# na_in's attention scores as f32r products of high and low halves, the queries' norm moved to where the scores are read

## What is computed

```python
def _heads(h, w, g=None):
    t = (h @ w).reshape(b, n, -1, HEAD_DIM)          # 16 heads of 64
    return t if g is None else _rms(t, g)            # t * rsqrt(mean(t*t) + EPS) * g

# queries of 256 tokens, keys and values of 256 + 256 (context)
s_loc = einsum(q_r, k_win) * scale + bias            # scale = 64 ** -0.5
s_ctx = einsum(q_r, k_ctx) * scale
p = softmax(concatenate([s_loc, s_ctx], axis=-1))
out = p_loc @ v_win + p_ctx @ v_ctx
```

## Time and profile before

| | us |
|---|---|
| median of 3 runs | 1310.28 |
| lowest and highest run | 1308.92, 1313.0 |
| the profiled execution, own time | 1312.8 |
| its span, first to last instruction | 1310.7 |
| mean granted TensorE clock | 0.997 of full |

### The profile page before, as it was taken

The page is one execution under the profiler, slowest core; times in us unless marked ns, Lnnn a source line. Parts: engine busy times, 40 slices in busy tenths (PEclk is TensorE's granted clock), DMA queues, the critical chain, the costliest instruction groups (busy, mean ns, idle before and its releaser), DMA issues.

```text
span 1310.7 us, 19842 instructions
## 1 busy us (share of the span) xinstructions
PE 1292.8 (99%) x7748; PEld 1102.5 (84%) x7748; DVE 868.7 (66%) x1303; ACT 594.8 (45%) x955; POOL 430.9 (33%) x433
## 2 busy tenths in 40 slices
PE   9999999999999999999999999999999999999999
PEld 8887989999886888788788888887777777999987
DVE  6687688999966588798333543335667666855553
ACT  6236556666653223354311234223555554766432
POOL 1462232333320002365300244111457552488200
PEclk9999999999999999999999999999999999999999
DMA  8777566555655344554444444444522321655552
GB/s 302 238 266 255 170 204 203 183 181 189 199 187 209 137 160 137 177 180 163 155 145 145 145 145 145 141 147 162 193 80 98 113 81 54 203 178 184 187 192 81
DMA packets 66268, 219.97 MB, mean 168 GB/s; under 512 B 9120, under 2 KB 12448, under 8 KB 66176
## 3 DMA queue, kind: packets, MB, share of 16 engines
q1 hardware_dynamic: 65888, 218.46, 49.3%
q10 hardware_dynamic: 288, 0.25, 0.1%
HBM read 217.21 MB, written 1.05 MB: 167 GB/s over the span
## 4 chain that ended last, share of the span: by engine, by line
PE 76%; DVE 13%; issue 5%; ACT 3%; DMA 2%; POOL 1%; SPq 0%; DVEq 0%; ACTq 0%; POOLq 0%
PE ps L624 19%; PE ps L638 18%; PE ps L636 18%; PE ps L614 7%; PE ps L616 4%; DVE wlo L1713 4%; DVE tmp L2003 2%; DMA raw<-in_w_in 2%; PE ps L1074 1%; DVE Y L1740 1%; PE ps L1101 1%; PE ps L1088 1%; ACT A L1258 1%; PE ps L1067 1%; PE ps L739 1%
## 5 line engine op out<-in xcount | busy, mean ns | idle before, releaser
L624 PE MATMUL ps<-A,whi 128*128 128x256 f32 (+2 forms) x1564 | 513.0, 328 | 0.2 <-ACT A L1490 0.2
L638 PE MATMUL ps<-A,wlo 128*128 128x256 f32 (+2 forms) x1536 | 492.3, 320 | 2.1 <-DVE wlo L1713 2.1
L636 PE MATMUL ps<-A,whi 128*128 128x256 f32 (+2 forms) x1536 | 491.9, 320 | 0.2 <-DVE A L1726 0.2
L1713 DVE TENSOR_TENSOR wlo<-raw,whi 128x1024 fp32r<-128x1024 f32 (+1 forms) x302 | 393.3, 1306 | 88.4 <-ACT whi L1233 88.2
L1233 ACT ACTIVATE whi<-raw 128x1024 fp32r<-128x1024 f32 (+1 forms) x302 | 316.7, 1051 | 266.9 <-PE ps L638 137.6
L624 PEld LDWEIGHTS ps<-A,whi 128*128 128x128 f32 x1564 | 297.9, 190 | 43.4 <-issue 18.4
L638 PEld LDWEIGHTS ps<-A,wlo 128*128 128x128 f32 x1536 | 292.6, 191 | 23.9 <-DVE wlo L1713 2.9
L636 PEld LDWEIGHTS ps<-A,whi 128*128 128x128 f32 x1536 | 293.1, 191 | 22.0 <-issue 1.7
L2394 POOL TENSOR_TENSOR H<-tmp,H 128x256 fp32r<-128x256 f32 (+1 forms) x86 | 125.8, 1462 | 56.4 <-ACT H L1548 42.9
L614 PE MATMUL ps<-H,whi 128*128 128x512 f32 x400 | 140.3, 395 | 0.2 <-POOL H L2394 0.2
L616 PE MATMUL ps<-H,wlo 128*128 128x256 f32 x400 | 112.3, 281 | 0.6 <-DVE wlo L1713 0.6
(11 more groups left out here) (321 smaller groups left out, 1496.9 us busy)
## 6 DMA issues: line engine op xcount, KB each, us to landing
raw<-in_ada SPq DMA_DIRECT2D x96, 512.0 KB, 4.3
raw<-in_w SPq DMA_DIRECT2D x64, 512.0 KB, 3.5
raw<-in_w_up SPq DMA_DIRECT2D x44, 512.0 KB, 3.5
raw<-in_w_in SPq DMA_DIRECT2D x34, 512.0 KB, 5.7
raw<-in_w_0a SPq DMA_DIRECT2D x32, 512.0 KB, 3.7
raw<-in_w_0b SPq DMA_DIRECT2D x32, 512.0 KB, 3.5
raw<-in_na_in SPq DMA_DIRECT2D x24, 512.0 KB, 5.7
raw<-in_w_down SPq DMA_DIRECT2D x22, 512.0 KB, 3.5
```

The source lines that it names most:

```text
L624: e.matmul(o, w_hi, ah, start=k == 0, stop=False)
L636: e.matmul(o, w_hi, al, start=False, stop=False)
L638: m = e.matmul(o, w_lo, ah, start=False, stop=last)
L1713: e.tensor_tensor(wlo[i % NRAW][:, :cols], raw[i % NRAW][:, :cols], plain(whi[s % NHI][:, :cols]), SUB).then_inc(S("wlo").sem, 1)
```

## The change

The scores of a head are made from f32r halves. A tile q_both holds 512 columns: in the columns of head x its own 64 rows hold the high half of the unscaled queries, and the other 64 rows the low half. k_hi holds the high half of the head's keys in all 128 rows (the same values twice), k_lo the low half in the head's own rows and zeros in the others. One product with k_hi and one with k_lo, both 128 rows deep, give high by high, low by high and high by low.

The queries are no longer multiplied by their norm and gain. Both gains go into the keys (head_gain), and the queries' root is a column for the 128 queries of a block (query_scale): their sum of squares is taken with the squares as weights and two columns of the ones matrix, and the scale is applied where VectorE reads the scores. VectorE makes that root's Newton step itself on four columns.

ScalarE writes the high halves: two copies for the queries at their chunk, four for the keys three chunks later (keys_hi). VectorE subtracts the queries' low half from PSUM one chunk later (queries_lo), and the bank of a query chunk now waits for that too. GpSimd makes the keys' Newton step and scales the keys (key_newton) at the following chunk, and subtracts their low halves (keys_lo) three chunks later, in the program behind the key_newton of that place. k2 has two tiles in place of three. Before the stage, VectorE clears the other rows of k_lo and makes the two gain columns.

The diff, with comments and places of tiles cut:

```diff
...
     cv = h32("cv", 2048, 40960).rearrange("p (c t) -> p c t", c=4)
-    k2 = [h32(f"k2_{i}", 512, 2048 * i) for i in range(3)]
-    q2 = [h32(f"q2_{i}", 256, 6144 + 1024 * i) for i in range(3)]
+    k2 = [tmp[1], tmp[3]]
+    q_both = [sb(f"q_both{i}", 512, f32r, at=h_at + at) for i, at in enumerate((0, 2048, 4096))]
+    key_places = [51200 + 2048 * i for i in range(7)] + [6144]
+    k_hi, k_lo = [[[sb(f"{what}{c}{x}", 512, f32r, at=h_at + key_places[4 * c + 2 * y + x]) for x in range(2)] for c in range(2)]
+                  for y, what in enumerate(("k_hi", "k_lo"))]
     v2 = [h32(f"v2_{i}", 512, 9216 + 2048 * i).rearrange("p (t c) -> p t c", t=4) for i in range(3)]
...
             return None
-        return (2 * c, k2[c % 3], 512) if kind == "k" else (2 * c + 1, q2[c % 3], 256)
+        return (2 * c, k2[c % 2], 512) if kind == "k" else (2 * c + 1, q_both[c % 3], 256)
     turn2 = {}
...
                 turn2["scores", 4 * p + 2 * b + x] = len(turn2)
+    query_mean, head_gain = small[:, 24:28], small[:, 40:42]
+    key_mean, key_root = (tmp[0], rst), (tmp[2], ssum)
+    def query_scale(p):
+        return small[:, 28 + 4 * (p % 3):32 + 4 * (p % 3)]
+    def key_at(n):
+        return NA_CHUNKS[n][1] if 0 <= n < 24 and NA_CHUNKS[n][0] == "k" else None
+    def query_at(n):
+        return NA_CHUNKS[n][1] if 0 <= n < 24 and NA_CHUNKS[n][0] == "q" else None
     GROUPS = (range(5), range(5, 9), range(9, 13))
...
                 w.wait_ge(S(signal), count)
+                if name == "na_in" and query_at(n - 3) is not None:
+                    w.wait_ge(S("q_lo"), 2 * query_at(n - 3) + 2)
         def low_ready(s):
...
             w.wait_ge(S("na"), n + 1)
-            o = turn_bank("norm", j)[:, :T]
-            e.matmul(o, const("blocks"), src, start=True, stop=True).then_inc(S("hn_sum").sem, 1)
+            o = turn_bank("norm", j)
+            if j % 2 == 0:
+                e.matmul(o[:, :T], const("blocks"), src, start=True, stop=True).then_inc(S("hn_sum").sem, 1)
+                return
+            for b in range(2):
+                m = e.matmul(o[:, 2 * b:2 * b + 2], src[:, 128 * b:128 * b + 128], const("blocks")[:, 0:128:64],
+                             start=True, stop=True)
+            m.then_inc(S("hn_sum").sem, 1)
         def scores2(p, b):
-            w.wait_ge(S("hn_out"), 2 * p + 2)
+            w.wait_ge(S("k_hi"), 4 * p + 4)
+            w.wait_ge(S("k_lo"), 2 * p + 2)
+            w.wait_ge(S("q_lo"), 2 * p + 2)
+            w.wait_ge(S("key_zero"), 4)
             for x in range(2):
                 o = turn_bank("scores", 4 * p + 2 * b + x)
-                e.matmul(o, q2[p % 3][rows_of(x), 128 * b:128 * b + 128], k2[p % 3][rows_of(x), :],
-                         start=True, stop=True).then_inc(S("s2_mm").sem, 1)
+                both = q_both[p % 3][:, 256 * x + 128 * b:256 * x + 128 * b + 128]
+                e.matmul(o, both, k_hi[p % 2][x], start=True, stop=False)
+                e.matmul(o, both, k_lo[p % 2][x], start=False, stop=True).then_inc(S("s2_mm").sem, 1)
         def turned2(p, b):
...
         def head_root(j, T):
-            m, r = tmp[j % 2][:, :T], tmp[2 + j % 2][:, :T]
+            m, r = (query_mean, query_scale(j // 2)) if j % 2 else (key_mean[j // 2 % 2], key_root[j // 2 % 2])
             w.wait_ge(S("na_bank"), turn2["norm", j] + 1)
-            if j >= 2:
-                w.wait_ge(S("hn_out"), j - 1)
+            if j % 2 == 0 and j >= 4:
+                w.wait_ge(S("hn_out"), j // 2 - 1)
             e.activation(r, m, ACT.Ln).then_inc(S("hn_ln").sem, 1)
...
             e.activation(r, r, ACT.Exp, scale=-0.5).then_inc(S("hn_exp").sem, 1)
+        def keys_hi(c):
+            w.wait_ge(S("hn_out"), c + 1)
+            if c >= 2:
+                w.wait_ge(S("s2_mm"), 4 * (c - 2) + 4)
+            for x in range(2):
+                e.activation(k_hi[c % 2][x][rows_of(x)], k2[c % 2][rows_of(x)], ACT.Copy).then_inc(S("k_hi").sem, 1)
+            for x in range(2):
+                e.activation(k_hi[c % 2][x][rows_of(1 - x)], k2[c % 2][rows_of(x)], ACT.Copy).then_inc(S("k_hi").sem, 1)
         def exp2(p, b):
...
                     sqr = sq[j % 2]
-                    if c >= 3:
-                        w.wait_ge(S("s2_mm"), 4 * (c - 3) + 4)
-                    e.activation(dst, o[:, :T], ACT.Copy).then_inc(S("na_copy").sem, 1)
+                    if j % 2:
+                        if c >= 3:
+                            w.wait_ge(S("s2_mm"), 4 * (c - 3) + 4)
+                        for x in range(2):
+                            e.activation(dst[rows_of(x), half(x)], o[rows_of(x), :T], ACT.Copy).then_inc(S("q_hi").sem, 1)
+                    else:
+                        if c >= 2:
+                            w.wait_ge(S("k_lo"), 2 * c - 2)
+                        e.activation(dst, o[:, :T], ACT.Copy).then_inc(S("na_copy").sem, 1)
                     if c:
...
                     e.activation(tmp[4], o, ACT.Copy).then_inc(S("na").sem, 1)
+                if key_at(n - 3) is not None:
+                    keys_hi(key_at(n - 3))
             if what == "after":
...
             ada_place(i)
+        for c in range(2):
+            for x in range(2):
+                e.memset(plain(k_lo[c][x][rows_of(1 - x)]), 0.0).then_inc(S("key_zero").sem, 1)
+        for i, factor in enumerate((-0.5, 1.5)):
+            e.scalar_tensor_tensor(head_gain[:, i:i + 1], param("k_g"), factor, param("q_g"), MUL, MUL).then_inc(S("head_gain").sem, 1)
         def head_mean(j, T):
             w.wait_ge(S("hn_sum"), j + 1)
-            if j >= 2:
-                w.wait_ge(S("hn_rr"), j - 1)
             bank = ps[4 + turn2["norm", j] % 2]
-            e.tensor_scalar(tmp[j % 2][:, :T], bank[:, :T], 1.0 / 64, EPS, MUL, ADD).then_inc(S("na_bank").sem, 1)
-        def head_out(j, T, dst, gain):
-            c, kind = j // 2, j % 2
-            w.wait_ge(S("hn_rr"), j + 1)
-            w.wait_ge(S("na_copy"), j + 1)
-            e.scalar_tensor_tensor(dst, dst, gain, tmp[2 + j % 2][:, :T], MUL, MUL).then_inc(S("hn_out").sem, 1)
+            if j % 2:
+                if j > 1:
+                    w.wait_ge(S("hn_q"), j // 2)
+                e.tensor_scalar(query_mean, bank[:, 0:4], 1.0 / 64, EPS, MUL, ADD).then_inc(S("na_bank").sem, 1)
+                return
+            if j >= 4:
+                w.wait_ge(S("hn_out"), j // 2 - 1)
+            e.tensor_scalar(key_mean[j // 2 % 2], bank, 1.0 / 64, EPS, MUL, ADD).then_inc(S("na_bank").sem, 1)
+        def queries_lo(c, n):
+            o, into = bank_of("na_in", n), q_both[c % 3]
+            w.wait_ge(S("q_hi"), 2 * c + 2)
+            w.wait_ge(S("na"), n + 1)
+            for x in range(2):
+                e.tensor_tensor(into[rows_of(1 - x), half(x)], o[rows_of(x), :256], plain(into[rows_of(x), half(x)]),
+                                SUB).then_inc(S("q_lo").sem, 1)
+        def query_newton(c):
+            m, r = query_mean, query_scale(c)
+            w.wait_ge(S("hn_exp"), 2 * c + 2)
+            for _ in range(2):
+                e.tensor_tensor(m, m, r, MUL).then_inc(own.sem, own.up())
+                w.wait_ge(own, own.n)
+            e.tensor_scalar(m, m, -0.0625, 0.1875, MUL, ADD).then_inc(own.sem, own.up())
+            w.wait_ge(own, own.n)
+            e.tensor_tensor(r, r, m, MUL).then_inc(S("hn_q").sem, 1)
         def values_out(c):
...
                 m = small[:, 8 + 4 * i:9 + 4 * i]
+                scale = query_scale(p)[:, 2 * b + x:2 * b + x + 1]
+                w.wait_ge(S("hn_q"), p + 1)
                 w.wait_ge(S("s2_mm"), j + 1)
...
                 bank = ps[4 + turn % 2]
-                e.scalar_tensor_tensor(X[x][:, 0:256], bank[:, 0:256], 0.125, bt[h % 4][:, b], MUL, ADD).then_inc(S("na_bias").sem, 1)
-                e.tensor_scalar(X[x][:, 256:512], bank[:, 256:512], 0.125, None, MUL, ALU.bypass).then_inc(S("na_bank").sem, 1)
+                e.scalar_tensor_tensor(X[x][:, 0:256], bank[:, 0:256], scale, bt[h % 4][:, b], MUL, ADD).then_inc(S("na_bias").sem, 1)
+                e.tensor_scalar(X[x][:, 256:512], bank[:, 256:512], scale, None, MUL, ALU.bypass).then_inc(S("na_bank").sem, 1)
                 w.wait_ge(S("na_bank"), turn + 1)
...
         def during_na(n):
-            if norm2(n - 2):
-                j, dst, T = norm2(n - 2)
-                head_out(j, T, dst, param("q_g" if j % 2 else "k_g"))
             if norm2(n - 1):
...
                 head_mean(j, T)
+            if query_at(n - 1) is not None:
+                queries_lo(query_at(n - 1), n - 1)
+            if query_at(n - 2) is not None:
+                query_newton(query_at(n - 2))
             written("na_in", n)
...
         shifted_lo("na", 1, 0)
-        def head_newton(j, T):
-            m, r = tmp[j % 2][:, :T], tmp[2 + j % 2][:, :T]
-            w.wait_ge(S("hn_exp"), j + 1)
+        latest = [(S("na_lp"), 4)]
+        def key_newton(c):
```

(30 more changed lines are left out.)

## The result

The changed kernel took 1315.17 us (median of 8 runs, 1313.0 to 1317.44) against 1310.01 for the kernel before (8 runs): a ratio of 1.0033, with an interval of 1.0024 to 1.0042 (the ratio is not taken from the two medians alone, which would give 1.0039). By the medians it is 5.2 us slower, by the ratio 4.3; it is not 1.4 faster. The profiled execution took 1315.91 us, 1314.1 from its first to its last instruction.

What follows compares the result with a forecast made beforehand. TensorE was taken as the bound, busy 1292.8 of 1310.7 us. From 1310.28: start +0.4, up to (1,0) -0.1, clock +1.7, its pairs -0.5, up to (3,0) +0.5, rest -3.4, total -1.4, giving 1308.9 us; range 1303.5 to 1313.5.

Steps and rivals of the forecast that it cites:

- TensorE idle 3 to 4 us ahead of pair (1,0): Sign of being right: this wait before head pair 1, query block 0, released by GpSimd's k_lo.
- 1.5 to 3.5 ahead of (3,0): Sign of being right: TensorE idle this many us before head pair 3, query block 0.
- rival (b): Waits for the keys' halves don't occur, as half-row subtractions cost half or GpSimd is ahead; 1301.2 us, chance 0.16.
- +0.4: Stage start: k_lo clears and two tiny products on VectorE delay wlo of unit 2; 0 to 0.9 us, taken as 0.4.
- -0.1: Start of pair (1,0): wait of 2.8 to 4.5 us swallows earlier gains; -0.9 to +0.8 us, taken as -0.1.
- 957.8: Time in us when VectorE starts key 2's mean, with head_out gone and pair (0,1) leaving about 1 us earlier.
- +0.5: Stretch (2,0) to (3,0): wait of 1.4 to 3.4 us for key 3's halves; -0.5 to +1.5, taken as +0.5.
- -3.4: Remaining pairs: seven plain -1.7, (4,1) -0.5, (5,1) and (6,1) -1.4, query sums +0.2 us.
- After it, each of the five banks is free before its second head: Waits inside five score pairs vanish, as VectorE loses head_out and the queries' mean shrinks to four columns.
- I take one such drop behind it: +1.7.: Clock falls once behind the wait before (1,0), that wait being longer than an earlier 2.28 us one; +1.7 us.
- 0.24: Gain in us per undisturbed score pair on TensorE: four f32r products take 0.92 instead of 1.16; eleven pairs 2.6.
- Rival (c): GpSimd and VectorE block each other at each meeting, three a chain; +4.2 us, 1314.5 us, chance 0.13.

Runs made afterwards that it cites:

- e1: Changed kernel with GpSimd's keys_lo ahead of key_newton at each chunk; 1306.28 us, ratio 0.9962 to the kernel before.
- e8: Changed kernel with keys_lo ahead of key_newton at chunk 6 only, for key 1; 1309.75 us, ratio 0.999 to the kernel before.
- e7: Changed kernel with only key 1's Newton step one chunk later, keys_lo order kept; 1313.06 us, ratio 1.0017 to the kernel before.
- e0_after: Changed kernel timed again without any edit; 1315.28 us, ratio 1.0033 to the kernel before.
- e4: Changed kernel with thrown-away products filling the waits, 18 ahead of (1,0) and 10 ahead of (3,0); 1313.61 us, ratio 1.002 to the kernel before.
- e5: e2 with scores as one plain f32 product of 64 rows per head, low halves made but unused; 1308.31 us, ratio 0.9977 to the kernel before.
- b1: Kernel before, with only head_mean put ahead of head_out on VectorE; 1306.37 us, ratio 0.9969 to the unedited kernel before.
- e2: Changed kernel with keys_lo first, as in e1, and each key's Newton step one chunk later; 1301.84 us, ratio 0.9929 to the kernel before.
- e3: Changed kernel with 18 thrown-away products ahead of the wait before (1,0) only; 1316.0 us, ratio 1.0035 to the kernel before.

## Why the prediction was wrong, point by point

**The places were right.** "TensorE idle 3 to 4 us ahead of pair (1,0)", "1.5 to 3.5 ahead of (3,0)", for the reason given, keys_lo behind the next key's Newton step: 4.43, above what was said, and 2.56. e1 takes both away, e8 the first alone. The durations on GpSimd were right too: half-row subtractions go by columns (2.59 for two, 1.30 each, as in the "1.30" of the text), so the condition of rival (b) did not hold. keys_hi on ScalarE was no cause: on GpSimd the halves of key 1 stood behind the Newton step, not behind ScalarE, whose last copy of key 1 ended at 964.5.

In the forecast's own terms the table says: start +0.8 against "+0.4"; up to (1,0) +2.8 against "-0.1"; (1,0) to (2,0) +2.6 against +1.2, the drop less the gain of two pairs; up to (3,0) +2.5 against "+0.5"; the rest -3.0 against "-3.4". Of the 7.1 us between, 2.9 and 2.0 lie in the two stretches that end with late halves.

**The step that failed: "957.8", key 2's mean.** The forecast had it 1 us earlier because (0,1) would leave VectorE sooner, 11.45 us after (0,0) (957.8 - 946.35). It came 14.05 after it, 2.6 late. What follows was nearly as forecast: mean to Newton 2.10 (2.09), Newton with its gaps 6.95 (6.1 to 6.9), 0.17 of waiting and the two subtractions 2.59. The 2.6 go straight into "(1,0) ... I take -0.1", which measured +2.8. Its parts: the wlo at 949.65 took 2.15 beside the longer Newton step of key 1, 0.95 more than in e7; the scores of (0,1) then waited 0.95 for X, which GpSimd's probabilities held behind that same step. e7 took both away and gave back 1.75 of the 2.6. The other 0.9 are mostly two terms that "957.8" left out. The subtractions of the queries' low halves stand ahead of the scores of (0,1) (0.88 at 951.90); the forecast counted them for key 4 and not here. And the eight readings of (0,0) and (0,1) take 0.48 with a column as scale, 0.41 before, together 0.5. Against them VectorE began to read (0,0) 0.72 us after its start, 1.16 before. So the step that failed is the time of key 2's mean, and with it the forecast that the gains up to (1,0) would balance the wait. What I had not done is to ask, for the step I lengthened by 1.3 us, who waits behind it *at key 1*; I asked it for key 3 only ("the pair (2,1) needs X back from the probabilities").

**"(2,0) to (3,0) +0.5", measured +2.5.** The mechanism was stated, its size was off: key 4's mean came at 1003.26, 14.9 after (2,0) ("13.0 to 14.2"), the Newton step took 7.0, and the pair started 26.9 after (2,0) ("23.8 to 25.8"). VectorE waited for X here as well, in the timeline of the changed kernel:

```profile
998.08 0.48 DVE L2354 SCALAR_TENSOR_TENSOR X<-ps,small,bt 128x256 f32<-128x256 f32 x1 [1.60 <-POOL Y L2647]
```

**"After it, each of the five banks is free before its second head".** Wrong at (0,1): 0.92 for the queries' mean, whose 0.15 us stood behind the wlo of 2.15. And I looked at score products alone, where a key's sum of squares is just as much a user of these banks: 0.65 and 1.72 at L1089. They did not add to the path where a large wait followed, which is why (0,0) to (1,0) cost 2.8 and not more.

**The clock.** "I take one such drop behind it: +1.7." The drop was there. It cost 2.9 in this profile, 2.6 in e7 (10.19 from (1,0) to (1,1)) and 1.6 in e0_after, so the size was right for one profile and too small for the others; in the median the clock is worth about 1.7 by e4. "Behind (3,0) ... as likely as not": it fell in two of the five profiles with that wait, in both after it had held behind (1,0).

**The small terms held or were off by little.** Start "+0.4": +0.8. The four clears are in the timeline of VectorE, 0.64 apart:

```profile
922.74 0.48 DVE L2299 MEMSET k_lo<- 64x512 f32 x1 [0.16 <-issue]
923.38 0.48 DVE L2299 MEMSET k_lo<- 64x512 f32 x1 [0.16 <-issue]
```

2.6 us against the 2 of slack make the 0.54 of waiting, within "0 to 0.9". "Rest -3.4": -3.0. "0.24" a pair: the undisturbed pair (2,0) gave more. In the changed kernel the transposes and the pair run from 987.57 to 989.38, 1.81 us:

```profile
987.57 1.04 PE L1119 MATMUL ps<-con,Y 128*128 128x128 f32 x8
988.37 0.48 PE L1105 MATMUL ps<-k_hi,q_both 128*128 128x512 f32 x1
988.68 0.40 PE L1106 MATMUL ps<-k_lo,q_both 128*128 128x512 f32 x1
988.91 0.40 PE L1105 MATMUL ps<-k_hi,q_both 128*128 128x512 f32 x1
989.14 0.39 PE L1106 MATMUL ps<-k_lo,q_both 128*128 128x512 f32 x1
989.38 0.39 PE L643 MATMUL ps<-A,whi 128*128 128x512 f32 x1
```

In the kernel before the same transposes start at

```profile
983.50 1.03 PE L1088 MATMUL ps<-con,Y 128*128 128x128 f32 x8
```

and the second product behind the pair at 985.86, so the first one began 0.23 earlier in effect: 2.13. The gain is 0.32, and 0.33 to 0.40 by e5. I had priced the pair from its first record on and so left out the handing over to 64-row products: from the start of the transposes to the pair's first record it is 0.97 before and 0.80 now. The Trainium skill (TensorEngine Tiling (Array Packing), Key Properties) says that a change of the tiling mode drains the engine; the trace agrees with the 0.17 us between these two.

**Rival (c) was the nearest,** 1314.5 for GpSimd and VectorE in each other's way. What happened is a mixture: its mechanism at one meeting ahead of (1,0) and at two Newton products (3.50 instead of 2.65), and the queue behind the longer Newton step, on which (c) put 0.5 and which held the scores of (0,1) for 0.95. That its 1314.5 comes so near is in part luck: it contains a second drop of the clock, which the changed kernel's profiles do not have. The Trainium skill (SBUF — State Buffer, SBUF: two separate sides) calls the shared ports an exclusive lock for a whole instruction; the 2.15 us of a wlo that takes 1.20 without the Newton step beside it agree.

**The balance at full clock.** The profiles at a clock of 1.0 compare without drops: b1 1303.0 us, e1 1302.5, e2 1298.2, e4 1310.0; the changed kernel with its waits filled is 11.8 us above e2. The waits of more than 0.6 us in the changed kernel's rows add up to 11.0 (0.92, 0.65, 4.43, 1.72, 2.56, 0.69; in e4 itself the 1.72 is 0.66), which is nearly all of it; the clock comes on top. Against the kernel before, e2 gains 8.9, in the medians (1310.78 to 1301.84) and in the stage (187.8 to 178.9) alike. In the stage 5.3 of it are the form, and 3.6 are there without it (187.8 to 184.3 in e5). b1, the swap alone, has 182.9. So the rest of the change costs 1.4 us even where nothing waits for the halves, 0.8 of them ahead of (0,0), where the wait for wlo is 0.53 (by the medians of b1 and e5 1.9, with rounds on different chips).

## What to carry to other kernels

When a step on a side engine gets longer, list all that is queued behind it on that engine at each of its occurrences, and for each ask which engine waits for it; the first occurrence can differ from the one you looked at. Put what the bounding engine needs next ahead of what it needs later: here the order alone decided between 0.3% slower and 0.4% faster (e1), and one more step moved made it 0.7% (e2). And before pricing a gain to a change, see whether part of it (here the waits in the pairs) can be had by a swap in the old kernel.

## What was not expected of the hardware

The same idle time of TensorE had different consequences: behind 2.56 us before (3,0) the clock held in the profile of the changed kernel, behind 2.55 it fell in that of e8, and in e3 behind 2.57; it fell where it had held behind (1,0). A drop behind 4.43 us lasted 6.8 us, one behind 4.42 in the same kernel 3.4. Tiny VectorE operations took longer beside GpSimd as well; in e2_newton_late the queries' Newton products on four columns, beside the end of GpSimd's Newton step of key 1 and the probabilities, took 0.65 us each instead of 0.17:

```profile
956.46 1.30 DVE L2329 TENSOR_TENSOR small<-small 128x4 f32<-128x4 f32 x2
957.80 0.66 DVE L2331 TENSOR_SCALAR small<-small 128x4 f32<-128x4 f32 x1
```
